# Second mixer of a three-layer transformer kernel: the modulation's sums move from TensorE to ScalarE and GpSimd

## What is computed

```
mod = silu(c) @ ada_w[1] + ada_b[1]            # c: (1, 1024), ada_w[1]: (1024, 6144)
shift1, scale1, gate1, shift2, scale2, gate2 = split(mod, 6)
h = rms(x, norm1_w[1]) * (1 + scale1) + shift1
q, k, v = split(h @ w_in, 3)                    # w_in: (1024, 3072), 8 heads of 128
q, k = rms(q) * q_norm, rms(k) * k_norm
x = x + gate1 * (attention(q, k, v, rel_bias) @ w_out)
x = x + gate2 * experts(rms(x, norm2_w[1]) * (1 + scale2) + shift2)
```

## Time and profile before

| what | us |
|---|---|
| median of 3 runs | 2108.6 (2108.18 to 2110.26) |
| the profiled execution | 2113.38 |
| its span in the trace | 2111.6 |
| second mixer in the trace, to the last output projection | about 701 to 870 |
| the experts behind it | about 870 to 1345 |

### The profile page before, as it was taken

One profiled execution on the slowest core, in us unless ns is written; L12 is line 12 of the kernel. 1 busy time (PEld: TensorE's weight loads), 2 busy tenths in 40 slices (PEclk: granted clock), 3 DMA queues, 4 the chain that ended last, 5 costly groups with the idle time before them and its releaser, 6 DMA issues. The chain is left out here.

```text
span 2111.6 us, 28565 instructions
## 1 busy us (share of the span) xinstructions
PE 1937.1 (92%) x11309; PEld 995.9 (47%) x11309; DVE 555.6 (26%) x1279; ACT 366.4 (17%) x819; POOL 3.1 (0%) x7
## 2 busy tenths in 40 slices
PE   5998999988988799999999888899999999998987
PEld 1443555544444345555544444455555555544443
DVE  1143522222112223622211122323553311111112
ACT  1141310000000223310000000214322211111111
POOL 0000000000000000000000000000000000000000
PEclk7999999999999999999999999999999999999999
DMA  8958799999999774899999999832327899999996
GB/s 307 308 193 324 288 425 422 426 426 424 426 424 416 255 272 164 341 388 424 424 425 425 427 424 426 278 123 83 118 80 294 370 422 424 426 425 425 425 427 263
DMA packets 128884, 727.80 MB, mean 345 GB/s; under 512 B 19272, under 2 KB 25627, under 8 KB 79659
## 3 DMA queue, kind: packets, MB, share of 16 engines
q1 hardware_dynamic: 125810, 725.14, 85.1%
q10 hardware_dynamic: 3002, 1.64, 0.4%
HBM read 724.91 MB, written 1.84 MB: 344 GB/s over the span
## 5 line engine op out<-in xcount | busy, mean ns | idle before, releaser
L286 PE MATMUL psum<-arena,norm_w 128*64 128x256 f32 x6144 | 702.0, 382 | 52.3 <-DMA arena<-in_moe_w_dram 31.9
L286 PEld LDWEIGHTS psum<-arena,norm_w 128*64 128x64 f32 x6144 | 434.8, 137 | 318.1 <-issue 56.2
L317 PE MATMUL psum<-arena,hT 128*64 128x512 f32 x1536 | 351.3, 599 | 34.1 <-DMA arena<-in_moe_w_dram 21.6
L393 DVE TENSOR_TENSOR hT<-psum,arena 64x512 f32<-64x512 f32 x128 | 88.1, 689 | 521.3 <-PE psum L317 520.4
L317 PEld LDWEIGHTS psum<-arena,hT 128*64 128x64 f32 x1536 | 107.7, 137 | 244.0 <-issue 221.1
L476 ACT ACTIVATE hT<-psum 128x256 f32<-128x256 f32 x96 | 36.8, 383 | 1006.3 <-PE psum L286 1006.3
L337 PE MATMUL psum<-hT 128*128 128x512 f32 x384 | 177.6, 605 | 7.7 <-DVE hT L393 6.0
L2268 PE MATMUL psum<-arena,hT 128*128 128x512 f32 (+1 forms) x352 | 153.8, 587 | 0.0
L337 PEld LDWEIGHTS psum<-hT 128*128 128x128 f32 x384 | 69.0, 189 | 97.9 <-issue 85.0
L713 DVE COPY hT<-psum 128x256 f32<-128x256 f32 x96 | 40.7, 424 | 263.6 <-PE psum L305 263.6
L2268 PEld LDWEIGHTS psum<-arena,hT 128*128 128x128 f32 x352 | 65.5, 193 | 67.8 <-issue 65.7
(11 more groups left out here) (417 smaller groups left out, 1241.0 us busy)
## 6 DMA issues: line engine op xcount, KB each, us to landing
arena<-in_moe_w_dram SPq DMA_DIRECT2D x192, 2048.0 KB, 37.6
arena<-in_w_gate_dram SPq DMA_DIRECT2D x32, 2048.0 KB, 32.5
arena<-in_w_up_dram SPq DMA_DIRECT2D x32, 2048.0 KB, 33.4
arena<-in_w_down_dram SPq DMA_DIRECT2D x32, 2048.0 KB, 30.9
arena<-in_ada_w_dram SPq DMA_DIRECT2D x24, 2048.0 KB, 13.3
arena<-in_w_in_dram SPq DMA_DIRECT2D x10, 2048.0 KB, 8.1
arena<-in_odd_w_in_dram SPq DMA_DIRECT2D x6, 2048.0 KB, 9.4
arena<-in_even_w_in_dram SPq DMA_DIRECT2D x4, 2048.0 KB, 17.4
```

The costliest lines, as they stand in the source:

```text
L286: m = nc.tensor.matmul(out[64 * half:64 * half + 64, :], xw[:, u, c, :], w[:, c, half * HALF:(half + 1) * HALF], start=(c == 0), stop=(c = ...
L317: m = nc.tensor.matmul(bank_Y[64 * half:64 * half + 64, :], hTs[:, k % 2, (k // 2) * 64:(k // 2) * 64 + 64], experts.slots[slot][2][:, k, ...
L393: return nc.vector.tensor_tensor(y[BLOCK * u:BLOCK * (u + 1), half, :], bank_Y[rows, :], gate2[rows, half * 512:half * 512 + 512], ALU.mult)
```

## The change

The modulation's sums over chunks leave TensorE. Of the 8 chunks of a block, GpSimd multiplies chunks 0 to 3 by the matching column of c, in place, and ScalarE chunks 4 to 7. GpSimd then adds the bias row into partition 0 of chunk 0, waits for ScalarE, and adds the chunks pairwise: 2048, 1024 and 512 elements per partition, the last into `part`. TensorE keeps `whole(i)`, with a constant of ones in place of `quads`; it now sums over all 128 partitions. The M items fall out of `SIDE_1`, so banks go to other items; the release of a slot and the load of block i + 2 hang on the GpSimd sum and are placed at ("W", i). `Chain` makes GpSimd wait for its own instruction before the next.

```diff
-SIDE_1 = (("P", 0, 0), ("P", 0, 1), ("M", 0), ("P", 1, 0), ("W", 0), ("M", 1), ("P", 1, 1), ("W", 1), ("M", 2), ("P", 2, 0), ("W", 2),
-          ("P", 2, 1), ("M", 3), ("P", 3, 0), ("W", 3), ("P", 3, 1), ("M", 4), ("P", 4, 0), ("W", 4), ("M", 5), ("P", 4, 1), ("W", 5),
-          ("M", 6), ("P", 5, 0), ("W", 6), ("P", 5, 1), ("M", 7), ("W", 7))
+SIDE_1 = (("P", 0, 0), ("P", 0, 1), ("P", 1, 0), ("W", 0), ("P", 1, 1), ("W", 1), ("P", 2, 0), ("W", 2), ("P", 2, 1), ("P", 3, 0), ("W", 3),
+          ("P", 3, 1), ("P", 4, 0), ("W", 4), ("P", 4, 1), ("W", 5), ("P", 5, 0), ("W", 6), ("P", 5, 1), ("W", 7))
...
         @block.gpsimd
         def _(pool):
-            nc.gpsimd.memset(btile, 0.0).then_inc(zeroed, 1)
+            link = Chain(pool, mod_step)
+            for i in range(len(mods)):
+                slot = slots[:, i % 2]
+                pool.wait_ge(mod_landed[i % 2], 32 * (i // 2 + 1))
+                for c in range(HC):
+                    m = nc.gpsimd.tensor_scalar(slot[:, c], slot[:, c], ccol[:, c:c + 1], None, ALU.mult)
+                link(m)
+                link(nc.gpsimd.tensor_tensor(slot[0:1, 0], slot[0:1, 0], btile[:, i % 2], ALU.add))
+                pool.wait_ge(mod_scaled, i + 1)
+                link(nc.gpsimd.tensor_tensor(slot[:, 0:4], slot[:, 0:4], slot[:, 4:8], ALU.add))
+                link(nc.gpsimd.tensor_tensor(slot[:, 0:2], slot[:, 0:2], slot[:, 2:4], ALU.add))
+                if i >= 2:
+                    wait_made(pool, "W", i - 2)
+                nc.gpsimd.tensor_tensor(part[:, i % 2], slot[:, 0], slot[:, 1], ALU.add).then_inc(mod_summed, 1)
...
-                if item[0] == "M" and item[1] + 2 < len(mods):
-                    wait_kept(sp, *item)
+                if item[0] == "W" and item[1] + 2 < len(mods):
+                    sp.wait_ge(mod_summed, item[1] + 1)
                     load_mod(item[1] + 2)
-            wait_kept(sp, "M", 6)
-            wait_kept(sp, "M", 7)
+            sp.wait_ge(mod_summed, len(mods))
...
-            def modulate(i):
-
-                pe.wait_ge(mod_landed[i % 2], 32 * (i // 2 + 1))
-                bank_free("M", i)
-                for c in range(2):
-                    for g in range(4):
-                        m = nc.tensor.matmul(side_bank("M", i)[32 * g:32 * g + 32, :], crep[:, 2 * g + c, :], slots[:, i % 2, 2 * g + c, :],
-                                             start=(c == 0), stop=(c == 1), skip_group_check=True)
-                m.then_inc(made[place["M", i] % 2], 1)
-
             def whole(i):
 
-                wait_kept(pe, "M", i)
+                pe.wait_ge(mod_summed, i + 1)
                 bank_free("W", i)
-                nc.tensor.matmul(side_bank("W", i), quads, part[:, i % 2], start=True, stop=True).then_inc(made[place["W", i] % 2], 1)
+                nc.tensor.matmul(side_bank("W", i), consts["ones"][:, :], part[:, i % 2], start=True, stop=True).then_inc(made[place["W", i] % 2], 1)
...
+            def scale_mod(i):
+
+                act.wait_ge(mod_landed[i % 2], 32 * (i // 2 + 1))
+                for c in range(HC, DC):
+                    m = nc.scalar.activation(slots[:, i % 2, c], slots[:, i % 2, c], ACT.Copy, scale=ccol[:, c:c + 1])
+                m.then_inc(mod_scaled, 1)
```

More of the change, by code:

```diff
@@ L3474, in middle_mixer_stage @@
     ss, rs = arena.take([2, 2, TILES, G]), arena.take([2, 2, TILES, G])
-    wq, wk, crep, quads = arena.take([P]), arena.take([P]), arena.take([DC, 32]), arena.take([P])
+    wq, wk = arena.take([P]), arena.take([P])
     assert arena.at <= 20130
@@ L3481, in middle_mixer_stage @@
     PT = arena.take([2, 2 * G, P])
-    part, btile = arena.take([2, MB]), arena.take([2, MB])
+    part, btile = arena.take([2, MB]), arena.take([2, MB], parts=1)
     slots = arena.take([2, DC, MB])
@@ L3487, in middle_mixer_stage @@
     made, kept = [sem("made0"), sem("made1")], [sem("kept0"), sem("kept1")]
-    small_landed, zeroed, mod_landed, crep_made = sem("small"), sem("zeroed"), [sem("mod0"), sem("mod1")], sem("crep")
+    small_landed, mod_landed, mod_step, mod_scaled, mod_summed = (
+        sem("small"), [sem("mod0"), sem("mod1")], sem("mod_step"), sem("mod_scaled"), sem("mod_summed"))
+    HC = DC // 2
     squared, root_asked, root_done, k_ready, q_ready, k_turned, q_turned, k_copied, q_copied = (
@@ L3526, in load_mod @@
                 sp.dma_start(slots[:, i % 2], m.wv[:, :, cols]).then_inc(mod_landed[i % 2], 16)
-                sp.dma_start(btile[0:1, i % 2], m.b[:, cols]).then_inc(mod_landed[i % 2], 16)
+                sp.dma_start(btile[:, i % 2], m.b[:, cols]).then_inc(mod_landed[i % 2], 16)
             for n in range(ring.AHEAD, ring.SLOTS):
                 ring.load(sp, n)
-            sp.wait_ge(zeroed, 1)
             load_mod(0)
             load_mod(1)
-            for dst, src in ((quads, w["quads"]), (wq, w["q_norm"].partition_broadcast(P)), (wk, w["k_norm"].partition_broadcast(P))):
+            for dst, src in ((wq, w["q_norm"].partition_broadcast(P)), (wk, w["k_norm"].partition_broadcast(P))):
                 sp.dma_start(dst, src).then_inc(small_landed, 16)
@@ L3648, in _ @@
                 project(0, t)
-            pe.wait_ge(crep_made, 1)
-            modulate(0)
             project(1, 0)
-            pe.wait_ge(small_landed, 48)
             whole(0)
-            modulate(1)
             project(1, 1)
             whole(1)
-            modulate(2)
             project(2, 0)
@@ L3660, in _ @@
             project(2, 1)
-            modulate(3)
             pe.wait_ge(k_ready, 1)
@@ L3672, in _ @@
             score(1)
-            modulate(4)
             turn_unit(0)
@@ L3676, in _ @@
             whole(4)
-            modulate(5)
             turn_unit(1)
@@ L3680, in _ @@
             whole(5)
-            modulate(6)
             output_unit(0)
@@ L3696, in _ @@
             score(3)
-            modulate(7)
             turn_unit(2)
@@ L3778, in _ @@
                 m.then_inc(open_act, 1)
+            scale_mod(0)
             keep(0, 0)
+            scale_mod(1)
             keep(0, 1)
@@ L3787, in _ @@
                 square(q, qT, 1, t, 0)
+            scale_mod(2)
             finish(1)
@@ L3790, in _ @@
             keep(2, 0)
+            scale_mod(3)
             finish(2)
@@ L3794, in _ @@
                 square(k, kT, 2, t, 1)
+            scale_mod(4)
             keep_heads(0, 6)
@@ L3801, in _ @@
                 square(q, qT, 3, t, 1)
+            scale_mod(5)
             keep_turned(0)
@@ L3808, in _ @@
             keep(4, 1)
+            scale_mod(6)
             finish(5)
@@ L3811, in _ @@
             keep(5, 0)
+            scale_mod(7)
             finish(6)
@@ L3823, in _ @@
             link = Chain(dve, step)
[L3825 to L3830, removed]
             def heads(ap, s, t):
@@ L3906, in _ @@
                 m.then_inc(open_dve, 1)
-            nc.vector.tensor_copy(crep, ccol.unsqueeze(2).to_broadcast([P, DC, 32])).then_inc(crep_made, 1)
-            dve.wait_ge(small_landed, 48)
+            dve.wait_ge(small_landed, 32)
             link(nc.vector.tensor_tensor(wk, wk, wq, ALU.mult))
-            add_bias(0)
             reduce_squares(kT, 0, 0, 0)
-            add_bias(1)
             link(reduce_squares(qT, 1, 0, 2))
             ask(0)
-            add_bias(2)
             norm_heads(0)
-            add_bias(3)
             reduce_squares(kT, 0, 1, 4)
@@ L3934, in _ @@
             scale(3)
-            add_bias(7)
             normalise(3)
@@ L4024, in program @@
     middle_mixer_stage(nc, ring, x, h, hT, dict(
-        q_norm=ins["c_q_norm"][0], k_norm=ins["c_k_norm"][0], norm2=ins["norm2_w"][1], quads=const_dram["quads"]), opening, mod,
+        q_norm=ins["c_q_norm"][0], k_norm=ins["c_k_norm"][0], norm2=ins["norm2_w"][1]), opening, mod,
         [(modulations[1], j) for j in (4, 5, 8, 9, 6, 7, 10, 11)], skewed, norm_w, ccol, consts, arena, psum, banks, plan,
```

4 lines of the change are left out of this document (removed).

## The result

The kernel after takes 2124.97 us, median of 4 runs (2123.9 to 2128.32), against 2109.26 for the kernel before: a ratio of 1.0077 with a 95% interval of 1.006 to 1.0095, so 13 to 20 us slower. The forecast was 2105.3 with a range of 2097 to 2119. The profiled execution took 2124.57 us, its span is 2122.8.

The account below looks back on a forecast made before the run. TensorE's matmul chain bounds the mixer, whose end starts the transfer-bound experts. Removed 19.4 us less new 16.1 leaves 3.3 us, taken from the median 2108.6: 2105.3 us, range 2097 to 2119.

Parts of the forecast that it names:

- C: GpSimd's whole work on one modulation block, between weights landed and the product over partitions: 12.1 us.
- A: GpSimd's first part of a block, scalings and bias, 2560 elements, which can run while ScalarE scales: 5.0 us.
- B: GpSimd's second part of a block, the three pairwise additions, 3584 elements, needing both scaled halves: 7.1 us.
- Rival 3: GpSimd dearer than VectorE's dearest row, so blocks run back to back from 750.2: C = 16 gives 2117.5; chance 0.23.
- 809.9 + 2C: Forecast start in us of the mixer's last product over partitions, whole(7), as a function of C; 834.1 forecast.
- rival 2: VectorE's head normalisations and GpSimd's block 2 additions exclude each other: 4.1 us more waiting, 2109.4; chance 0.18.
- The slow clock: Low TensorE clock after the stall at block 2's product over partitions, charged once at 2.1 us.
- The blocks between are in time: Blocks 3 to 6 summed at 774.4, 786.5, 800.9, 817.7, before TensorE wants them at 781, 799, 808, 820.
- the 14.9 us that TensorE gives up: Eight removed `modulate` pieces of 1.86 us in the mixer, the most that TensorE can give.
- the stage as the place where the end is set, one for one: A mixer ending x us sooner starts the transfer-bound expert stage x us sooner.
- the landing of block 2: Block 2's weights, load issued at 733.85 as before, land at 750.2; its product over partitions then waits for GpSimd.
- block 7's load: Decides the last product over partitions: issued at 808.1 behind a ring load, it lands at about 822.

Follow-up runs that it names:

- e1_forms: Kernel after with GpSimd's scalings in other forms per block: by a constant, one of 2048, copies, one spread product; only times per instruction are given.
- e5: Kernel after without VectorE's twelve head normalisations, q and k left unnormalised: 2121.8 us in one execution.
- e2: Kernel after with GpSimd keeping only its last addition of 512; scalings, bias and first two additions left out: 2096.14 us, ratio 0.9925 to before.
- e6: Against the kernel after, VectorE alone forms the sums, without GpSimd or ScalarE, and block 2's product comes one projection later: 2095.69 us, ratio 0.992 to before.
- e3: Kernel after with GpSimd's four scalings replaced by one 2048-element product with c spread along the row: 2119.04 us, ratio 1.0039 to before.
- e8: Kernel after with GpSimd's four scalings replaced by four copies, near the assumed price per block: 2112.98 us, ratio 1.0004 to before.
- e7: Kernel after with block 2's product over partitions one projection later on TensorE and in SyncE's list: 2127.05 us in one execution.
- e9: Against the kernel after, VectorE alone forms the sums, with block 2's product left where the change has it: 2098.66 us, ratio 0.9941 to before.
- e11: The kernel after timed once more, unchanged: 2127.13 us, ratio 1.0073 to before.

## Why the prediction was wrong

- The step that failed is the price of GpSimd's block, C = A + B = 12.1 us; it is 15.9. A was put at 5.0 us and is 6.18 + 0.08 + 1.26 = 7.5; B was put at 7.1 and is 8.3. The upper bound, VectorE's dearest addition at 1.97 ns per element, was no bound for another engine: an addition of GpSimd takes 2.2 to 2.5 ns and its scaling 3.0 in the change's form. The estimate from the Trainium skill (GPSIMD Engine Reference, Performance versus the Vector engine) was right for the addition, 4497 ns against 4500 to 4530 here where VectorE does not interfere. It was wrong for the scaling: the Trainium skill (GPSIMD Engine Reference, Engine selection) calls one-input work roughly line-rate, and e1_forms shows a low price for the copy (0.57 us per 512) but not for the scaling (1.55).
- The way from C to the time was right in kind. Rival 3's formula, six blocks back to back from block 2's landing, gives with 15.9 us whole(7) at 750.2 + 95.4 = 845.6, or 139.7 into the mixer; measured 142.1. So the case that came is rival 3, which had a chance of 0.23. The missing 2.4 us are rival 2 in kind: GpSimd's six blocks took 97.9 us and not 95.2, and e5 shows 1.5 of it to be the head normalisations. The two were priced as if one or the other came. (A slip in the sum: 809.9 + 2C and 750.2 + 6C meet at C = 14.9, not at 14.5. At 15.9 it changes nothing.)
- The slow clock was charged once, behind W2. It was paid behind W7 as well: 2.9 us of the 13.6. By its own formula C = 15.9 makes the forecast 2116.9, still inside the range; that is 11.6 of the 16.9 us by which the mixer's length was missed. The 2.4 and the 2.9 make it 2122, outside the range that was drawn from rival 3 at C = 16.3 alone. The last 2.8 us of the measured time lie outside the mixer.
- "The blocks between are in time" held for W3 and W4 and failed for W5 and W6 (4.00 and 1.78 us); for W1 the wait is 4.85 in place of none. All follow from C.
- Right: the 14.9 us that TensorE gives up (14.7 in e2, some 13.7 in e6), the stage as the place where the end is set, one for one (the experts take 476.3 to 477.8 us in every kernel), the landing of block 2 at 44.3 us into the mixer (44.1 measured), block 7's load as the next bound (e3, e8).
- At the assumed price the walk would have missed by 3.6 us at W7 (e8), and the forecast gain of 3.3 us would not have come. The largest part, 2.4 us, is VectorE's division held up by GpSimd, which the prediction saw only for the head normalisations; those and the clock behind W2 make about 1.7.

## To carry to other kernels

An engine that has no row in the profile has no price: take its time from a run of that form, or let the bound reach past the dearest row of the other engines. A side chain that refills its own buffers is bound by blocks x time per block as soon as that exceeds what the main engine does between two of them; a wait on the main engine then tells the rate, and moving the wait gains next to nothing (e7). Where the chain is quick enough, moving it does gain: 6.5 us from e9 to e6. Price each engine for the very operation: VectorE took 6.6 us per block for what ScalarE and GpSimd together took 15.9.

## What the runs showed of the hardware

- GpSimd's time per element, 128 partitions of float32: copy 1.1 ns, product with a spread operand 1.76, addition 2.2 (2048 elements) to 2.5 (512), scaling by a constant or a column 2.6 to 3.0 (e1_forms and the kernel after). An addition of 512 on one partition takes the 1.26 us of one on 128. The kind of the operation counts for more than the number of its inputs.
- A VectorE instruction with two SBUF inputs that met an addition of 2048 elements on GpSimd lasted until its end (4.08 us in place of 0.69). So did one with a single input and 16 elements (3.34 in place of 0.17, e8); the Trainium skill (SBUF — State Buffer, Who interferes with whom) names `tensor_scalar` among the operations that can contend in a two-port mode. Beside GpSimd's scalings a two-input product kept its 1.22 us, and others lost at most 0.4 us.
- The length of TensorE's wait before W7 did not tell the clock behind it. Behind 2.91 us (e3, e8) and 4.8 us (after, e11) the product took 2.08 us, behind 3.47 us (e5) 1.13, with a granted clock of 1.00 in the row below of e5_no_heads. What decides between them stays open.

```profile
848.00:854.00 6.00, 5.95 (x25) 3.56 (x26) 1.87 (x3) 1.35 (x5) 0.00 (x0) 1.00 0.49 74
```
